# Expert layers that gather x in place with a step of eight values, x summed in PSUM, and five smaller edits

## Chip, cores and metric

One Trainium2 chip, one core. The metric is the device time of one launch in microseconds (us); lower is better. All arithmetic is float32. The program holds two layers with a mixture of experts (the first behind a convolution, the second behind an attention) and a third block with a state-space mixer, stick-breaking attention and a feed-forward network.

## The reference

The input has 256 tokens of 1024 values. The parts that the change touches, cut:

```python
ALPHA = (2.0 * DEPTH) ** 0.25            # DEPTH = 2
...
def grouped_moe(x, router_w, router_bias, w_gate, w_up, w_down):
    ...
    w = w / jnp.sum(w, -1, keepdims=True)
    gates = jnp.sum(jax.nn.one_hot(e_idx, N_EXPERTS, dtype=jnp.float32) * w[..., None], axis=1)
    def step(acc, ew):
        g_e, wg_e, wu_e, wd_e = ew
        h = jax.nn.silu(x2 @ wg_e) * (x2 @ wu_e)
        return acc + (h @ wd_e) * g_e[:, None].astype(x2.dtype), None
...
        x = layer_norm(ALPHA * x + mix, ln_mix_g[l], ln_mix_b[l])
        ffn = grouped_moe(x, router_w, router_bias, moe_w_gate[l], moe_w_up[l], moe_w_down[l])
        x = layer_norm(ALPHA * x + ffn, ln_ffn_g[l], ln_ffn_b[l])
```

There are 16 experts of width 512, and each token goes to two. The third block works on 272 positions, 16 learned ones ahead of the 256 tokens; only the tokens are put out, and its feed-forward convolution has three taps.

## The kernel before

A matmul keeps a stationary operand of up to 128x128 in TensorE (loaded by a weight load, PEld) and moves up to 512 columns past it. A float32 matmul shows in the trace as two records, each with its own weight load. `ring` is a ring of weight buffers in SBUF that the SP queue fills, `arena` is scratch, `x_nat` holds x with tokens in the partitions, `xT` the same turned. Banks 0 to 3 of PSUM go round by job (`take_bank`, `bank_free`, `job_ready`); banks 4 to 7 hold the sum over the experts. Each engine runs its own list in program order; semaphores tie them together. `normed`, `seats_ready`, `scattered` and the like are such semaphores.

**Convolution** (`conformer`). TensorE makes eight blocks of the gated product (`glu_products`, helper line 243); ScalarE writes each to DRAM (`send`, L928) and fetches it back in shifted form (`fetch_shifted`, L937, four DMAs); TensorE applies the taps (`taps`, L859) to it. Behind the last fetch, ScalarE's queue issues 17 small DMAs: the rows of the bias of the next product, router weights, and others that later stages need (L974 to L991, then `load_norm`, L496 and L498). Behind those stands `squares_of` (L951), on which TensorE's `square_part` (L876) waits. The normalization that follows works on 256 columns at a time: DVE takes a reciprocal (L522), subtracts and multiplies, ScalarE applies SiLU (L1000), and `project_and_turn` (L561) starts with the first of eight blocks.

**Routing** (`route`). TensorE makes the router's logits (L1167, L1173), DVE ranks them (L1123 to L1158) and TensorE counts places (L243 with `upto` and `ones`). Beside that ScalarE copies x twice: L1113 writes `by_row`, x with its 1024 values in another order (value 8f+k goes to place f of row k), and L1116 multiplies `x_nat` by ALPHA for the sum at the layer's end. The order is needed because the expert weights are loaded with eight rows of the matrix in each partition.

**Experts** (`experts`). The experts go in eight pairs. For a pair, `fetch` gathers its tokens: two jobs of four 128-column blocks, each block two matmuls with `by_row` as stationary operand and the seats (a 0/1 matrix of 128 tokens by 128 seats) as moving operand. So a pair's gather has 16 matmuls, 32 records and 32 weight loads. The list of one pair on TensorE is gate and up of side 0 (L1460), turning the seats (L1469), gate and up of side 1, `scatter` of the pair before (L1505, four matmuls of 512 columns), `turn` of the hidden values (L1479), gather of the next pair (L243), down (L1493). DVE's `hidden` (L1365) and ScalarE's copy of the turned values (L1428) stand between.

```python
    def gather(dst_at, tokens_dst, sources=seats):
        for c in range(4):
            k = dst_at * 4 + c
            last = products(tokens_dst[:, c * P:c * P + P],
                            [(by_row[:, t, k, :], sources[:, t, :]) for t in range(2)])
```

**Layer's end** (`ffn_norm`). DVE adds each of four 128x512 pieces of the sum to ALPHA x (`experts_sum`, L1096), takes its statistics (L1098), then centres and scales the two token tiles (L540 in layer 0, L613 and L615 in layer 1) for the transposes (L462).

**Third block.** `project_turned` (L681) multiplies 272-column operands in the z and output projections; `qk_products` (L243) makes q and k, also with 272 columns. The feed-forward stage already leaves out the first 14 positions (258 columns).

Of the kernel before, what the change touches and what calls it, by code (L numbers as in the profile page):

```python
# [24 lines left out]
F32 = mybir.dt.float32  # L25
# [23 lines left out]

IN_LAST = {x: n for n, x in enumerate(("GU0", "S", "GU1", "T", "Y0", "Y1"))}  # L50
# [13 lines left out]
FFN_TAPS = 3  # L64
OFF_XBC = D
# [81 lines left out]
def program(nc, a, out):  # L147
# [26 lines left out]
    eps_cols = sb("eps_cols", P, 2)  # L174
# [91 lines left out]
    def pair_job(layer, p, kind):  # L266
        return FJ[f"moe{layer}"] + 2 + PAIR_JOBS * p + (IN_LAST if p == PAIRS_E - 1 else IN_PAIR)[kind]

# [84 lines left out]

    block = ctx.enter_context(nc.Block())
# [5 lines left out]
    def _(sp):  # L360
# [41 lines left out]
        while u < len(units):  # L402
            src = units[u][0]
            if u == 1:

                sp.wait_ge(rows_cleared, 1)
                for q in range(QUADS):
# [4 lines left out]
                                     consts_loaded, 16)  # L412
            slot_freed(u)
# [16 lines left out]
    norm_count = [0, 0]  # L430
# [61 lines left out]
    def load_norm(k, gain, bias=None):  # L492

        act = nc.scalar
        norm_count[k % 2] += 32
        act.dma_start(norm_rows[:, k % 2, 0, :], gain.partition_broadcast(P)).then_inc(norm_loaded[k % 2], 16)  # L496
        b = gain if bias is None else bias
        act.dma_start(norm_rows[:, k % 2, 1, :], b.partition_broadcast(P)).then_inc(norm_loaded[k % 2], 16)  # L498

# [9 lines left out]
    def sqrt_of(act, values, scale, eps, table=True):  # L509
# [6 lines left out]
        bias = eps_cols[0:p, 0:1] if eps == LN_EPS else eps_cols[0:p, 1:2]  # L516
# [14 lines left out]
    def variance_of(k, t):  # L531

        nc.vector.wait_ge(stats_ready, 4 * k + 2 * t)
        nc.vector.bn_aggr(small[:, 2 * t:2 * t + 2], stats[:, t, :, :]).then_inc(var_ready, 1)

    def centred_scaled(t, root, normed, xhat=xhat):

        mean, var = mean_var(t)
        reciprocal_of(nc.vector, var, root)
        nc.vector.tensor_scalar(xhat[t - 1], x_nat[:, t, :], mean, var, ALU.subtract, ALU.mult).then_inc(normed, 1)  # L540
# [10 lines left out]
    def project_and_turn(first, u0, lhs, normed, ready=None):  # L551
# [3 lines left out]
        def part(j, half, t):  # L555
            unit_ready(u0 + half)
            take_bank(j)
            for k in range(KC):
                if ready is not None and j == first:
                    ready(k)  # L560
# [13 lines left out]
    def mix_norm(layer, normed, scaled):  # L574
# [7 lines left out]
        def _(dve):  # L582
            residual(first, 1, 0, scaled)
            residual(first + 1, 1, 1, scaled)
            variance_of(k, 1)
            centred_scaled(1, roots[0], normed)
# [3 lines left out]
            variance_of(k, 2)  # L590
            centred_scaled(2, roots[1], normed)
# [11 lines left out]
    def ffn_norm(layer, normed):  # L603
# [6 lines left out]
        def rows_out(t, root):  # L610
            dve, (mean, var) = nc.vector, mean_var(t)
            reciprocal_of(dve, var, root)
            dve_step(dve.scalar_tensor_tensor(x_nat[:, t, :], x_nat[:, t, :], mean, norm_rows[:, k % 2, 0, :],  # L613
# [5 lines left out]
        def _(dve):  # L619
            experts_sum(layer, 1, 0)  # L620
            experts_sum(layer, 1, 1)
            variance_of(k, 1)
            experts_sum(layer, 2, 0)
# [2150 lines left out]
```

## Time and profile before

| | |
|---|---|
| median of 3 runs | 1486.72 us (1485.76 to 1489.68) |
| profiled execution, its own time | 1485.41 us |
| its span, first to last instruction | 1483.7 us |
| granted TensorE clock over the span | 0.946 |
| TensorE busy / weight loads busy | 1357.4 us (91%) / 852.5 us (57%) |
| VectorE (DVE), ScalarE (ACT), GpSimd (POOL) busy | 384.4, 263.2, 24.6 us |
| share of TensorE in the chain that ended last | 88% |
| moved by DMA | 314.36 MB, mean 212 GB/s |

The profile is one execution. "Idle before" is how long an engine waited, and the arrow names what released it; "issue" is a wait for nothing that the profile shows, which can be a DMA. A matmul's busy time overlaps its neighbour's, so rates are read from the starts of merged pieces, not from mean durations.

### The profile page before, as it was taken

The numbers are of one execution on the slowest core, as the hardware profiler recorded it, in microseconds if no ns is written. First come the engines' busy times: TensorE is split into PE (matmuls) and PEld (weight loads), VectorE is DVE, ScalarE is ACT, GpSimd is POOL, SyncE is SP. The second block draws the span as 40 slices with busy tenths as digits, with TensorE's granted clock in tenths as the row PEclk, the third lists the DMA queues.
The fourth block names the chain that finished last, engine by engine and source line by source line (L and its number), as shares of the span: only waits on it lengthen the run. The fifth ranks groups of instructions, "written<-read, shape, count | busy, mean of one in ns | idle before, by whom it ended". The sixth has DMA issues, their size and how long they took to land.

```text
span 1483.7 us, 15495 instructions
## 1 busy us (share of the span) xinstructions
PE 1357.4 (91%) x6438; PEld 852.5 (57%) x6438; DVE 384.4 (26%) x857; ACT 263.2 (18%) x565; POOL 24.6 (2%) x49
## 2 busy tenths in 40 slices
PE   7979799999989978799999969988899996999997
PEld 6744434444347754434444358866686785888743
DVE  0013512112141332521112141465303205222201
ACT  1002311001102331311001121321325103000000
POOL 3110000000000000000000000000000000000000
PEclk9989799999999987799999979988999998999998
DMA  9960699999961050699999941311221033543420
GB/s 327 315 173 1 255 380 426 425 426 427 402 234 57 24 204 1 255 391 427 425 425 427 401 167 56 115 57 57 85 86 57 0 114 115 169 161 127 167 85 28
DMA packets 91663, 314.36 MB, mean 212 GB/s; under 512 B 9746, under 2 KB 47158, under 8 KB 77766
## 3 DMA queue, kind: packets, MB, share of 16 engines
q1 hardware_dynamic: 77344, 298.98, 52.0%
q10 hardware_dynamic: 14246, 14.33, 3.4%
q8 instruction: 55, 0.90, 0.3%
q14 instruction: 18, 0.15, 0.0%
HBM read 311.05 MB, written 2.24 MB: 211 GB/s over the span
## 4 chain that ended last, share of the span: by engine, by line
PE 88%; DVE 7%; DMA 1%; issue 1%; ACTq 1%; ACT 1%; DVEq 0%; SPq 0%; POOLq 0%
PE psum L243 37%; PE psum L1460 15%; PE psum L1493 8%; PE psum L681 6%; PE psum L2676 5%; PE psum L561 4%; PE psum L1505 4%; PE psum L462 1%; PE psum L859 1%; PE psum L1636 1%; PE psum L1634 1%; DMA ring<-in_a_w_pw 1%; PE psum L2334 1%; PE psum L2326 1%; PE psum L2321 1%
## 5 line engine op out<-in xcount | busy, mean ns | idle before, releaser
L243 PE MATMUL psum<-xT,ring 128*128 128x256 f32 (+2 forms) x1792 | 413.0, 392 | 8.8 <-POOLq L442 5.2
L243 PEld LDWEIGHTS psum<-xT,ring 128*128 128x128 f32 x1792 | 346.0, 194 | 72.4 <-issue 15.3
L1460 PE MATMUL psum<-ring,arena 128*64 128x512 f32 x768 | 169.6, 594 | 0.0
L1460 PEld LDWEIGHTS psum<-ring,arena 128*64 128x64 f32 x768 | 53.9, 137 | 103.9 <-issue 103.7
L243 PE MATMUL psum<-arena 128*128 128x128 f32 (+4 forms) x684 | 92.4, 291 | 1.2 <-issue 1.1
L243 PEld LDWEIGHTS psum<-arena 128*128 128x128 f32 (+2 forms) x684 | 84.1, 198 | 5.5 <-issue 4.8
L1493 PE MATMUL psum<-ring,arena 128*64 128x512 f32 x384 | 85.0, 595 | 0.0
L1365 DVE TENSOR_TENSOR arena<-psum,arena 64x512 f32<-64x512 f32 x32 | 34.3, 1073 | 191.5 <-ACT arena L1413 191.5
L2676 PE MATMUL psum<-ring,arena 128*128 128x512 f32 x176 | 75.7, 592 | 0.0
L1413 ACT ACTIVATE arena<-psum 64x512 f32<-64x512 f32 x32 | 18.9, 592 | 259.4 <-PE psum L1460 259.4
L561 PE MATMUL psum<-ring,arena 128*128 128x512 f32 x128 | 60.3, 632 | 4.5 <-ACT arena L1000 3.6
L1505 PE MATMUL psum<-arena 128*128 128x512 f32 x128 | 59.1, 605 | 1.8 <-DVE arena L1382 1.8
L681 PE MATMUL psum<-arena,ring 128*128 128x272 f32 x256 | 58.8, 392 | 0.0
L2676 PEld LDWEIGHTS psum<-ring,arena 128*128 128x128 f32 x176 | 33.4, 190 | 41.7 <-issue 41.6
L1460 PE MATMUL psum<-arena 128*64 128x512 f32 x192 | 56.6, 594 | 0.0
L462 PE MATMUL psum<-ident,arena 128*128 128x128 f32 (+1 forms) x136 | 23.3, 337 | 35.9 <-DVE arena L1835 22.2
L1493 PEld LDWEIGHTS psum<-ring,arena 128*64 128x64 f32 x384 | 26.5, 137 | 49.4 <-issue 48.0
L681 PEld LDWEIGHTS psum<-arena,ring 128*128 128x128 f32 x256 | 48.6, 190 | 10.0
L561 PEld LDWEIGHTS psum<-ring,arena 128*128 128x128 f32 x128 | 25.7, 204 | 37.0 <-issue 35.2
L1505 PEld LDWEIGHTS psum<-arena 128*128 128x128 f32 x128 | 23.0, 189 | 37.8 <-issue 34.3
L462 PEld LDWEIGHTS psum<-ident,arena 128*128 128x128 f32 (+1 forms) x136 | 20.5, 188 | 41.6 <-DVE arena L1835 23.3
L1382 DVE COPY arena<-psum 128x512 f32<-128x512 f32 x16 | 11.1, 692 | 109.4 <-PE psum L1493 109.4
(319 smaller groups left out, 1184.4 us busy)
## 6 DMA issues: line engine op xcount, KB each, us to landing
ring<-in_moe_w_gate SPq DMA_DIRECT2D x24, 2048.0 KB, 11.8
ring<-in_moe_w_up SPq DMA_DIRECT2D x24, 2048.0 KB, 15.9
ring<-in_moe_w_down SPq DMA_DIRECT2D x24, 2048.0 KB, 16.1
ring<-in_w_in SPq DMA_DIRECT2D x11, 2048.0 KB, 13.6
ring<-in_w_up SPq DMA_DIRECT2D x22, 1024.0 KB, 7.7
arena<-in_moe_w_gate SPq DMA_DIRECT2D x8, 2048.0 KB, 12.2
ring<-in_w_down SPq DMA_DIRECT2D x5, 2048.0 KB, 7.7
ring<-in_a_w_pw SPq DMA_DIRECT2D x8, 1024.0 KB, 10.9
```

The source lines that it names most:

```text
L243: last = nc.tensor.matmul(dst, lhsT, rhs, start=(n == 0), stop=(n == len(pairs) - 1))
L462: last = nc.tensor.transpose(bank(j)[:, c * P:c * P + n], src(t)[0:n, at:at + P], ident[0:n, 0:n])
L561: last = pe.matmul(bank(j), lhs(k, t), slot_k(u0 + half)[:, k, :], start=(k == 0), stop=(k == KC - 1))
L681: last = nc.tensor.matmul(bank(first + c)[:, 0:L], slot_k(part_units[half])[:, k, (c % 4) * P:(c % 4) * P + P], src[:, k, :], start=(i == ...
L859: last = pe.matmul(bank(j)[32 * g:32 * g + 32, 0:SEQ], blocks[:, c % BLOCK_BUFS, q, g, :], shifted[:, c % REP_BUFS, g, 4 * q:4 * q + SEQ], ...
L1365: dve.tensor_tensor(hid_both[part, :].rearrange("s (k f) -> s k f", f=P), by_row(bank(j)[part, :]), by_row(silu_g[part, 0, :]), ALU.mult). ...
L1413: act.activation(silu_g[UP_IN[side], 0, :], bank(j)[GATE_IN[side], :], ACT.Silu).then_inc(silu_ready, 1)
L1460: last = pe.matmul(bank(j)[part, :], tokens[:, k, side * SEATS:side * SEATS + SEATS], weights(u + n, k), start=(k == 0), stop=(k == KC - 1))
L1493: last = pe.matmul(bank(j)[part, :], hidT_both[:, k, side * SEATS:side * SEATS + SEATS], weights(u + side, k, D)[:, half * 512:half * 512 ...
L1505: last = pe.matmul(psum[:, BANKS + 2 * t + half, :], gatedT[:, p % 2, t * P:t * P + P], y_pair[:, half * 512:half * 512 + 512], start=Fals ...
L1634: pe.matmul(bank(j)[:, comp * SEQ:comp * SEQ + keys], flip, bias[:, h, SEQ - keys:SEQ], start=True, stop=False)
L2676: last = pe.matmul(psum[:, BANKS + 2 * t + half, :], fT[:, c, t * P:t * P + P], slot_k(u, D)[:, c % 4, half * 512:half * 512 + 512], start ...
```

## The change

1. **Gather in place.** `by_row` and ScalarE's copies into it are gone. The stationary operand of each gather matmul is x_nat itself with a step of eight values (32 bytes).
2. **x summed in PSUM.** In `route`, four matmuls of 512 columns with the identity put x into banks 4 to 7; the experts add to them, with gates divided by ALPHA. The copy with ALPHA and DVE's memset of the banks are gone. At the layer's end DVE reads statistics and values straight from PSUM; epsilon is divided by ALPHA squared.
3. **Order within the pairs.** In the first pair the gather of the next stands ahead of `turn`. In the last, two of the four scatter matmuls stand behind it. The last scatter takes the left halves of both tiles first, and waits for each half's copy by itself.
4. **Small DMAs.** The 17 DMAs go from ScalarE's queue to SP's, ahead of the loads of pw2, the next projection.
5. **Halves in the convolution's norm.** DVE and ScalarE work on 128 columns at a time; the second tile's columns have their own waits.
6. **Third block.** The first 14 of 272 columns are left out of z, q, the output projection and the products between.

```diff
+            if u == unit_at["pw2"]:
+                sp.dma_start(b_pw2, a["a_b_pw2"][0].partition_broadcast(P)).then_inc(bias_rows_loaded, 16)
+                sp.wait_ge(consts_made, CONSTS_MADE)
...
+                load_norm(0, a["ln_mix_g"][0], a["ln_mix_b"][0], sp)
             slot_freed(u)
...
-                                        src[:, k, :], start=(i == 0 and k == 0),
+                                        src[:, k, NEED:L], start=(i == 0 and k == 0),
...
-            for c in range(KC):
-                act.wait_ge(conv_normed, c + 1)
-                act.activation(conv[:, c, :], conv[:, c, :], ACT.Silu, bias=column("a_ln_b", c),
-                               scale=column("a_ln_g", c)).then_inc(act_ready, 1)
+            for t in range(2):
+                for c in range(KC):
+                    act.wait_ge(conv_normed, KC * t + c + 1)
+                    part = conv[:, c, t * P:t * P + P]
...
-        dve_step(dve.tensor_tensor(x_nat[:, t, cols], x_nat[:, t, cols], psum[:, BANKS + 2 * (t - 1) + half, :],
-                                   ALU.add))
-        dve.bn_stats(stats[:, t, half, :], x_nat[:, t, cols]).then_inc(stats_ready, 1)
+        dve.wait_ge(scattered, 4 * layer + 2 * half + t)
+        dve.bn_stats(stats[:, t, half, :], psum[:, BANKS + 2 * (t - 1) + half, :]).then_inc(stats_ready, 1)
...
-            for t in range(2):
-                act.wait_ge(normed[2 * layer], 3 + t)
-                act_step(act.activation(by_row[:, t, :, :], x_nat[:, t + 1, :].rearrange("p (f k) -> p k f", k=KC),
-                                        ACT.Copy))
-            act.nop().then_inc(rows_ready, 1)
-            act.activation(x_nat[:, 1:3, :], x_nat[:, 1:3, :], ACT.Copy, scale=ALPHA).then_inc(rows_ready, 1)
...
+            for t in (1, 2):
+                pe.wait_ge(normed[2 * layer], 2 + t)
+                for half in range(2):
+                    pe.matmul(psum[:, BANKS + 2 * t - 2 + half, :], ident[:, :], x_nat[:, t, half * 512:half * 512 + 512],
+                              start=True, stop=False, skip_group_check=True)
             take_bank(J + 2)
...
+            by_dim = x_nat[:, 1:3, :].rearrange("p t (f k) -> p t k f", k=KC)
             last = products(tokens_dst[:, c * P:c * P + P],
-                            [(by_row[:, t, k, :], sources[:, t, :]) for t in range(2)])
+                            [(by_dim[:, t, k, :], sources[:, t, :]) for t in range(2)])
...
-            dve.memset(psum[:, BANKS:2 * BANKS, :], 0.0).then_inc(cleared, 1)
...
-                if p == 1:
-                    pe.wait_ge(cleared, layer + 1)
-                if p > 0:
-                    scatter(p - 1)
-                turn(p)
-                if p < LAST:
-                    fetch(0, p + 1)
-                    fetch(1, p + 1)
+                if p == 0:
+                    fetch_next(p)
+                    turn(p)
+                elif p < LAST:
+                    scatter(p - 1, TOP + LOWER)
+                    turn(p)
+                    fetch_next(p)
+                else:
+                    scatter(p - 1, TOP)
+                    turn(p)
+                    scatter(p - 1, LOWER)
                 down(p)
-            scatter(LAST)
+            scatter(LAST, ((0, 0), (1, 0), (0, 1), (1, 1)))
```

How the lists move, at two places. TensorE from the router to the first pair's hidden values of layer 0 (chosen rows, in order), before (L243 is the shared helper; `arena` holds `by_row`, the seats and the tokens):

```order
L1173 MATMUL psum<-quad_diag,arena 128x16 [waits bank_free3,bank_free0]
L243 MATMUL psum<-arena,upto 128x16 [waits won_ready,bank_free2,bank_free1]
L243 MATMUL psum<-arena 128x128 [waits bank_free3,seats_ready,rows_ready]
L1460 MATMUL psum<-ring,arena 64x512 x15
L1479 MATMUL psum<-ident,arena 128x128 [waits bank_free3,bank_free1,bank_free0]
L243 MATMUL psum<-arena 128x128 [waits bank_free1,seats_ready]
```

and now:

```order
L1181 MATMUL psum<-quad_diag,arena 128x16 [waits bank_free3,bank_free0]
L1188 MATMUL psum<-x_nat,ident 128x512 [waits normed0]
L1188 MATMUL psum<-x_nat,ident 128x512
L245 MATMUL psum<-arena,upto 128x16 [waits won_ready,bank_free2,bank_free1]
L245 MATMUL psum<-arena,x_nat 128x128 [waits bank_free3,seats_ready,normed0]
L245 MATMUL psum<-arena,x_nat 128x128 [waits bank_free0,seats_ready]
L1494 MATMUL psum<-ident,arena 128x128 [waits bank_free3,bank_free1,bank_free2]
```

The identity matmuls stand ahead of the wait for `won_ready`, and the second gather ahead of the turn. ScalarE from the last fetch on, before (L974 is the first of the 17 DMAs, L951 the squares) and now (L975 the squares, L1007 SiLU):

```order
L937 DMA arena<-glu_scratch 32x4x284 x4
L974 DMA arena<-in_a_b_pw 128x1024
L976 DMA router_w<-in_router_w 128x8x16
L978 DMA router_b<-in_router_bias 128x16
L980 DMA ffn_cols<-in_ln_ffn_g 128x8x1
```

```order
L961 DMA arena<-glu_scratch 32x4x284 x4
L975 ACTIVATE arena<-arena 128x256 x8
L547 ACT_TABLE_LOAD
L553 ACTIVATE xT<-xT,eps_cols 128x256
L1002 ACT_TABLE_LOAD
L1007 ACTIVATE arena<-arena,vec 128x128 x16
```

The squares follow the last fetch directly.

## Rows read from the trace of the kernel before

**Rows 1.** Chain in order of time, layer 0, pair 1: start us, us, what.
```profile
221.81 3.63 PE psum L1505 x8
225.88 3.57 PE psum L243 x32
...
254.80 3.57 PE psum L243 x32
```
**Rows 2.** Weight loads by line and form: xcount | busy us, mean ns | idle before.
```profile
L681 PEld LDWEIGHTS psum<-arena,ring 128*128 128x128 f32 x256 | 48.6, 190 | 10.0
L1460 PEld LDWEIGHTS psum<-ring,arena 128*64 128x64 f32 x768 | 53.9, 137 | 103.9 <-issue 103.7
```
**Rows 3.** ScalarE's instructions that read x_nat: duration ns min/median/max.
```profile
L1823 ACT ACTIVATE arena<-x_nat x6: 1040/1042/1057, 862.2 to 1239.6; 128x1024 f32<-128x1024 f32 x4, 16x1024 f32<-16x1024 f32 x2
L1113 ACT ACTIVATE arena<-x_nat x4: 2041/2050/2055, 166.6 to 612.9; 128x1024 f32<-128x1024 f32 x4
```
**Rows 4.** Windows of TensorE: length, busy (records), granted clock, DMA share, GB/s.
```profile
5.00:75.00 70.00, 64.60 (x408) 1.00 1.06 328
...
166.00:171.00 5.00, 0.47 (x3) 0.50 0.98 413
...
174.00:180.00 6.00, 6.00 (x34) 0.60 0.39 156
180.00:209.00 29.00, 27.13 (x143) 1.00 0.74 297
```
**Rows 5.** Timeline of TensorE, layer 0: counting places, first gather, first turn.
```profile
171.11 0.58 PE L243 MATMUL psum<-arena,upto 128*128 128x16 f32 x2 [4.64 <-DVE arena L1149]
...
173.93 6.12 PE L243 MATMUL psum<-arena 128*128 128x128 f32 x32 [0.54 <-issue]
...
196.32 0.63 PE L1479 MATMUL psum<-ident,arena 128*128 128x128 f32 x4 [1.87 <-DVE arena L1365]
```
**Rows 6.** Chain, convolution: squares, last taps, reciprocal.
```profile
106.45 2.93 PE psum L876 x6
...
115.89 3.59 PE psum L859 x64
...
123.01 1.76 DVE xT L522
```
**Rows 7.** Squares' matmuls as a group: xcount | busy us, mean ns | idle before.
```profile
L876 PE MATMUL psum<-arena,ones 128*128 128x256 f32 x16 | 5.8, 491 | 9.9 <-ACT arena L951 9.9
```
**Rows 8.** Chain, end of layer 0's experts: copy of the last output, transposes.
```profile
407.39 0.70 DVE arena L1382
...
417.60 1.97 PE psum L462 x8
```
**Rows 9.** Timeline of TensorE, down of layer 0's last pair.
```profile
400.27 2.33 PE L1493 MATMUL psum<-arena 128*64 128x512 f32 x9 [0.89 <-ACT arena L1428]
```
**Rows 10.** Timeline of DVE at the layers' ends: statistics, one rescaling pass.
```profile
410.16 0.69 DVE L1098 BATCH_NORM_STATS2 stats<-x_nat 128x6 f32<-128x512 f32 x1
...
857.75 1.28 DVE L613 SCALAR_TENSOR_TENSOR x_nat<-x_nat,small,norm_rows 128x1024 f32<-128x1024 f32 x1
```
**Rows 11.** Chain, layer 1: copy of the last output, last rescaling pass.
```profile
851.35 0.70 DVE arena L1382
...
863.80 1.28 DVE x_nat L615
```
**Rows 12.** Chain: output projection (272 columns), feed-forward (half 258, half 256).
```profile
1166.60 58.67 PE psum L681 x256
...
1245.43 152.77 PE psum L243 x704
```
**Rows 13.** DMAs of the second block's fetch (issued 38 to 40), us to landing.
```profile
DMA to landing us min/median/max: 6.3/10.3/22.4
```
**Rows 14.** Timeline of TensorE, the taps that wait for them.
```profile
62.52 3.66 PE L859 MATMUL psum<-arena 128*32 128x256 f32 x64 [0.88 <-issue]
```
**Rows 15.** DMA of ScalarE's queue, 92 to 108: packets, MB, share of 16 engines.
```profile
q10 hardware_dynamic: 6290, 2.30, 67.9%
```

More of the change, by code:

```diff
@@ L64 @@
 FFN_TAPS = 3
+NEED = META - (FFN_TAPS - 1)
 OFF_XBC = D
@@ L558, in part @@
             for k in range(KC):
-                if ready is not None and j == first:
-                    ready(k)
+                if ready is not None and half == 0:
+                    ready(k, t)
                 last = pe.matmul(bank(j), lhs(k, t), slot_k(u0 + half)[:, k, :], start=(k == 0), stop=(k == KC - 1))
@@ L680, in project_turned @@
                     for k in range(KC):
-                        last = nc.tensor.matmul(bank(first + c)[:, 0:L],
+                        last = nc.tensor.matmul(bank(first + c)[:, NEED:L],
                                                 slot_k(part_units[half])[:, k, (c % 4) * P:(c % 4) * P + P],
-                                                src[:, k, :], start=(i == 0 and k == 0),
+                                                src[:, k, NEED:L], start=(i == 0 and k == 0),
                                                 stop=(i == len(parts) - 1 and k == KC - 1))
@@ L783, in _ @@
             pool_step(pool.memset(eps_cols[:, 1:2], EPS))
+            pool_step(pool.memset(eps_cols[:, 2:3], LN_EPS / ALPHA ** 2))
             pool.nop().then_inc(consts_made, 1)
@@ L1496, in down, with scatter, fetch_next @@
                     last.then_inc(job_done, 1)
-            def scatter(p):
+            def scatter(p, parts):
                 read_out(pe, job("S", p))
-                read_out(pe, job("Y0", p))
-                read_out(pe, job("Y1", p))
-                for t in range(2):
-                    for half in range(2):
-                        last = pe.matmul(psum[:, BANKS + 2 * t + half, :], gatedT[:, p % 2, t * P:t * P + P],
-                                         y_pair[:, half * 512:half * 512 + 512], start=False, stop=(p == LAST),
-                                         skip_group_check=True)
-                        if p == LAST:
-                            last.then_inc(scattered, 1)
-            pe.wait_ge(rows_ready, 2 * layer + 1)
+                for t, half in parts:
+                    read_out(pe, job(f"Y{half}", p))
+                    last = pe.matmul(psum[:, BANKS + 2 * t + half, :], gatedT[:, p % 2, t * P:t * P + P],
+                                     y_pair[:, half * 512:half * 512 + 512], start=False, stop=(p == LAST),
+                                     skip_group_check=True)
+                    if p == LAST:
+                        last.then_inc(scattered, 1)
+            def fetch_next(p):
+                fetch(0, p + 1)
+                fetch(1, p + 1)
+            TOP, LOWER = ((0, 0), (0, 1)), ((1, 0), (1, 1))
+            pe.wait_ge(normed[2 * layer], 4)
             fetch(0, 0)
@@ L2367, in meta_exponents @@
                 zm = psum[:, META_BANK, :]
-                pe.matmul(zm[:, 0:L], neg_from_meta[:, :, :].rearrange("p h s -> p (h s)"), soft_meta[:, g, :], start=False, stop=True,
+                pe.matmul(zm[:, NEED:L], neg_from_meta[:, :, :].rearrange("p h s -> p (h s)"), soft_meta[:, g, NEED:L], start=False, stop=True,
                           skip_group_check=True)
@@ L2598, in _ @@
         def _(pe):
-            products(psum[:, BANKS, 0:L], [(ones[:, :], sqT[:, c, :]) for c in range(KC)]).then_inc(so_summed, 1)
+            products(psum[:, BANKS, NEED:L], [(ones[:, :], sqT[:, c, NEED:L]) for c in range(KC)]).then_inc(so_summed, 1)
             w = unit_at["w_out"]
```

211 lines of the change are left out of this document (110 added, 101 removed).

## The prediction

> **What bounds the kernel.** I read the page's engine shares first: TensorE is busy for 91% of the span and makes up 88% of the chain that ended last, so most of the time is matmuls, and a stage is judged by what stands between them. In the experts, the chain runs from TensorE to TensorE: one pair takes 254.80 - 225.88 = 28.92 us, with no wait of note in it [rows 1]. DMA moves 418 to 425 GB/s there on the page, yet no matmul waits for a weight. A gather is 3.57 us of that, 32 records at 112 ns each [rows 1]. Weight loads of 128 and of 64 columns last 190 and 137 ns [rows 2], which is 0.83 ns a column, so 128 columns occupy the load path for 107 ns of the 112. In the gather, load and matmul are thus about equally long: whatever lengthens a load shows at once. In most other stretches 512 columns pass per load and cover it.
>
> **Parts that gain.**
>
> The small DMAs. TensorE waits 9.9 us for the squares on ScalarE, whose queue first issues the 17 DMAs [rows 7]. With them gone the squares follow the last fetch, and the wait goes. The first six records then took 2.93 us [rows 6] at a reduced clock; by 217 ns for such a record (152.77/704) [rows 12] they need 1.3, so another 1.6. The DMAs don't disappear: on SP's queue they stand ahead of pw2 and of the first expert weights, which aren't needed for 100 us. What they can hurt is the convolution's own traffic (a rival below). Gain 11.5 us; ends 3 and 13.
>
> Halves in the norm. The reciprocal over 256 columns takes 1.76 us [rows 6] and stands before the first product; over half of them about 0.9, and multiply and SiLU shrink by some 0.3 together. The second halves are needed some 14 us later. Gain 1.2.
>
> First pair. The turn waited 1.87 us for the hidden values [rows 5]. The gather now fills that; what becomes exposed is ScalarE's copy of the turned values, 0.89 us as it shows in the last pair [rows 9]. Gain 1.0 a layer, 2.0.
>
> Last pair. Two scatter matmuls, half of 3.63 us [rows 1], cover that 0.89 [rows 9]; the other two still cover the hidden values. Gain 0.9 a layer, 1.8.
>
> Layers' ends. Counted from the start of the last copy, layer 0 reaches the decisive transposes after 417.60 - 407.39 = 10.2 us [rows 8]. Now the scatter starts at once with left halves and ends at 3.6; 0.3 for the semaphore, one statistics pass of 0.69 [rows 10] and 0.2 to combine give 4.8. Two centring passes from PSUM at about 1.28 [rows 10], with 0.17 for each reciprocal, end at 7.7. Gain 2.5. In layer 1 four passes follow: 4.8 + 4 x 1.28 + 0.4 = 10.3, against 863.80 + 1.28 - 851.35 = 13.7 [rows 11]. Gain 3.4. Together 5.9.
>
> Third block. A record took 58.67/256 = 229 ns with 272 columns and 217 with 257 on average [rows 12], 0.81 ns a column, so 14 columns are 11.4 ns. The trimmed records are 256 in the output projection, 128 each in z and q and some 36 others. 548 x 11.4 = 6.2; a few of q stand where TensorE waits for others, so 6.0. Ends 3 and 6.5.
>
> Sum of the gains: 11.5 + 1.2 + 2.0 + 1.8 + 5.9 + 6.0 = 28.4 us.
>
> **Parts at nothing or near it.** ScalarE's two copies of x, DVE's adds and the memset were beside the ranking and the first pair. If that cover were missing, the copies would already have delayed the first gather, which waits for the seats. New are four identity matmuls a layer: 8 records, 0.43 us each at the full clock and 0.86 at half (0.84 ns a column) [rows 12], so 3.4 to 6.9 us, in an idle time of 4.64 us [rows 5] at the half clock of 1.2 GHz (granted 0.50) [rows 4]. Behind them in TensorE's list are the counting matmuls, for which the seats wait. I take a delay of 0.5 us at the first gather; ends 0 and 2.3 a layer. TensorE is busy ahead of the gather now, so I expect the full clock of 2.4 GHz in it, where it was granted 0.60 [rows 4].
>
> **The step of eight.** No weight load in this trace reads with a step. From below its cost is nothing. The nearest rows are ScalarE's, on the same tensor with the same step: 1024 values in 2050 ns, against 1042 in order [rows 3]. That is 0.98 ns more a value, 128 x 0.98 = 126 ns a load. From above, the load might not only be longer but also stop overlapping its neighbour: 190 [rows 2] + 126 = 316 ns a record. I take the middle: the load path is occupied for 107 + 126 = 233 ns, with 2 for the handover 235 a record, since ScalarE too reads a value in 0.8 ns in order, at about the rate of the load. A gather becomes 32 x 235 = 7.5 us, 3.95 more. Of the 16, 14 stand in the full-clock chain: 55.3. The two first ones took 6.12 [rows 5] and start 0.5 later: 1.9 each, 3.8. Together 59.1 us, and nothing covers it, since the down products need the same TensorE.
>
> The Trainium skill ("SBUF — State Buffer", in the section on the DMA port swizzle) speaks against this change: SBUF is read in 16-byte lines, and an access that goes to a new line each time pays. By it, a step of 32 bytes pays on every value; it gives no price for a weight load, and ScalarE's row agrees with it.
>
> Sum against the profiled execution: 1485.4 - 28.4 + 59.1 = 1516.1. The median of the runs is 1.3 above that execution, so **1517 us**.
>
> **Rivals.**
>
> A: loads don't care about the step. What speaks for it: weight loads keep a rate of 0.83 ns a column over several shapes [rows 2], as if the array and not the memory set it, and TensorE may fetch ahead. Against: ScalarE's ratio of two. Then gathers stay at 3.57, and the two first ones gain the clock, 6.12 to 3.57 less 0.5, 2.0 each: 1485.4 - 28.4 - 4.1 + 1.3 = 1454 us. This is the other side; the point is a gather of 3.57 + 28.4/14 = 5.6 us, or 175 ns a record. Below it the kernel is faster. The Trainium skill ("TensorE: Matmul & The Clock Gate", section "LDWEIGHTS (loading the stationary operand)") gives a load as columns / 1.2 in ns, with nothing for the step; the slope in order agrees, and by it the time would be this rival's.
>
> B: the moved DMAs come back as waits. From 5 to 75 us the DMA engines are full (share 1.06) [rows 4]; the fetches of the second block land after up to 22.4 us [rows 13], and the taps behind them already wait 0.88 [rows 14]. In their old place ScalarE's DMAs took 67.9% of 16 us [rows 15], 10.9, about 8 of it the small ones. If those 8 land on the second block's taps, the convolution keeps only 5 of its 12.7: with the step's cost 1525 us. Against: most fetches have room, and the large loads move behind them.
>
> C: the loads no longer overlap, 316 ns a record: 10.1 us a gather, 92 for 14 and 9 for the first two, 42 more than forecast: 1559 us. A clock that falls during a sparse gather, so that the down products behind start at 1.2 GHz, would end in the same region. Against both: the loads of the present gather overlap, and no wait stands in it.
>
> D: the step costs a part, below 175 ns a record: 1460 to 1500.
>
> **Chances and range.** A measurement of this kernel can tell about 0.3% from no change, 4.5 us. Forecast 0.57 (its own range, from gains of 20 to 32 and a step's cost of 50 to 64: 1504 to 1530), A 0.22, B 0.09, C 0.06, D 0.06. Faster: A and half of D, 0.25. Same: 0.02, of D. Slower: 0.73. To leave out no more than 2 in 10 the range must reach to A and to B: 1448 to 1532.
>
> **What would show it.** Right: the gather's pieces of 32 records at 7.5 us in both layers; weight loads there at about 316 ns where others stay at 190; a pair of 32.9 us. The squares' wait of 9.9 gone, the squares at 96 to 97 us; layer 0's experts end 2.5 us sooner after the last copy; output projection at 218 ns a record, 55.8 us in all. Wrong: gathers at 3.6 us (A), a wait before the second block's taps of several us (B), gathers of 10 us or a granted clock below 1.00 between 180 and 400 us (C).

## The result and the profile after

| | before | changed |
|---|---|---|
| median | 1486.84 us (4 runs, 1485.76 to 1489.68) | 1514.52 us (4 runs, 1510.30 to 1517.53) |
| profiled execution, its own time | 1485.41 us | 1517.28 us |
| its span | 1483.7 us | 1515.6 us |
| granted TensorE clock | 0.946 | 0.959 |
| TensorE / weight loads busy | 1357.4 / 852.5 us | 1412.9 / 912.6 us |

The changed kernel takes 1.0181 of the time before (95% interval 1.0147 to 1.0215), so it is slower by 1.5 to 2.2%. The medians are 27.7 us apart. The changed kernel's profiled execution is 2.8 us above its median and the other 1.4 below, so the two spans, which what follows compares, are 31.9 us apart.

Weight loads as a group: xcount | busy us, mean ns | idle before. Loads of the same size in the third block's projections (L715) still take 190 ns, as in [rows 2].

```profile
L245 PEld LDWEIGHTS psum<-arena,x_nat 128*128 128x128 f32 x512 | 123.0, 335 | 3.6 <-issue 3.6
```

The chain that ended last, layer 0, pairs 1 and 2 (start us, us, what). It answers to [rows 1].

```profile
219.39 3.63 PE psum L1518 x8
223.46 7.61 PE psum L245 x32
...
256.41 7.61 PE psum L245 x32
```

A gather is 7.61 us, 238 ns a record, instead of 3.57 and 112. A pair is 256.41 - 223.46 = 32.95 us. The scatter keeps its 3.63. So the whole of the pair's growth of 4.03 us is the gather.

TensorE's timeline in the convolution (in brackets: idle before, and what released it). L883 is the taps, L900 the squares' matmuls, L597 the product that follows. It answers to [rows 6], [rows 7] and [rows 14].

```profile
82.16 3.66 PE L883 MATMUL psum<-arena 128*32 128x256 f32 x64
87.18 3.66 PE L883 MATMUL psum<-arena 128*32 128x256 f32 x64 [1.36 <-issue]
...
96.05 6.50 PE L883 MATMUL psum<-arena 128*32 128x256 f32 x64 [3.29 <-issue]
102.48 1.56 PE L900 MATMUL psum<-arena,ones 128*128 128x256 f32 x6
...
119.06 6.16 PE L597 MATMUL psum<-ring,arena 128*128 128x512 f32 x10 [2.59 <-ACT arena L1007]
```

The squares' wait of 9.9 us is gone, and so is the second block's 0.88. But the fifth and sixth taps now wait 1.36 and 3.29 us, and the sixth runs 6.50 instead of 3.66. The window of TensorE around it (length, busy, granted clock, DMA share, GB/s) shows half the clock, 1.2 GHz, after that wait:

```profile
95.00:100.00 5.00, 3.95 (x40) 2.21 (x44) 0.17 (x1) 0.71 (x3) 0.00 (x0) 0.50 0.54 140
```

The view of DMAs shows what the taps wait for. For the fetches issued between 62 and 82 us it has (xcount, KB each, median us to landing), and for the queue of SP's loads in the same stretch (packets, MB, share of 16 engines), first changed:

```profile
arena<-glu_scratch ACTq DMA_DIRECT2D x8, 142.0 KB, 18.3
q1 hardware_dynamic: 810, 6.99, 92.0%
```

and before:

```profile
arena<-glu_scratch ACTq DMA_DIRECT2D x12, 142.0 KB, 7.8
q1 hardware_dynamic: 145, 2.10, 30.0%
```

The fetches take more than twice as long, in a stretch in which SP's queue now moves 6.99 MB instead of 2.10.

TensorE's timeline in layer 0's routing: the identity matmuls, the first counting matmuls, the first two gathers [rows 5].

```profile
158.80 5.91 PE L1188 MATMUL psum<-x_nat,ident 128*128 128x512 f32 x8
164.54 0.29 PE L245 MATMUL psum<-arena,upto 128*128 128x16 f32 x2
...
166.66 7.84 PE L245 MATMUL psum<-arena,x_nat 128*128 128x128 f32 x32 [0.94 <-issue]
...
188.84 7.87 PE L245 MATMUL psum<-arena,x_nat 128*128 128x128 f32 x32
```

The chain at the layers' ends and in the third block. It answers to [rows 8], [rows 11] and [rows 12].

```profile
428.34 2.79 PE psum L1518 x6
433.01 1.34 DVE arena L576
434.46 1.35 DVE arena L576
436.28 3.59 PE psum L505 x16
439.88 41.51 PE psum L245 x128
...
902.31 2.79 PE psum L1518 x6
...
911.02 1.28 DVE x_nat L651
913.20 4.62 PE psum L505 x24
919.08 28.08 PE psum L715 x128
...
1201.37 55.68 PE psum L715 x256
...
1277.32 152.77 PE psum L245 x704
```

With the same events of before, the span divides like this. The forecast column is the prediction's terms put where they belong.

| stretch | before | changed | difference | forecast |
|---|---|---|---|---|
| to the first product after the convolution | 126.00 | 119.06 | -6.9 | -12.7 |
| from there to the first gather | 47.93 | 47.60 | -0.3 | +0.5 |
| first gather to v (layer 0's experts) | 245.64 | 273.22 | +27.6 | +24.7 |
| attention | 151.06 | 152.26 | +1.2 | 0 |
| layer 1's routing | 47.49 | 48.49 | +1.0 | +0.5 |
| first gather to z (layer 1's experts) | 253.77 | 278.45 | +24.7 | +23.8 |
| z to the feed-forward | 373.54 | 358.24 | -15.3 | -6.0 |
| the rest | 238.3 | 238.3 | 0 | 0 |

The parts sum to 32.0 against a forecast of 30.7 (59.1 - 28.4), but three rows are off by 3 to 9 us and largely cancel. The experiments are about these three and about the gather; attention's 1.2 us stay unexplained.

### The profile page after: what moved, and what is told of

It is laid out like the page before. It is cut to its first block, busy times and chain, and to the rows that moved or that the text cites. A ratio compares the mean times of both kernels' runs of the same rounds, so it can differ in the third digit from the quotient of the medians.

```text
span 1515.6 us, 15533 instructions
## 1 busy us (share of the span) xinstructions
PE 1412.9 (93%) x6454; PEld 912.6 (60%) x6454; DVE 378.5 (25%) x864; ACT 254.1 (17%) x569; POOL 25.1 (2%) x50
## 4 chain that ended last, share of the span: by engine, by line
PE 91%; DVE 5%; issue 1%; ACT 1%; DMA 1%; DVEq 0%; ACTq 0%; SPq 0%; POOLq 0%
PE psum L245 39%; PE psum L1475 15%; PE psum L1508 7%; PE psum L715 6%; PE psum L2700 5%; PE psum L597 4%; PE psum L1518 4%; PE psum L883 2%; PE psum L505 1%; PE psum L1658 1%; PE psum L1656 1%; PE psum L1188 1%; DMA ring<-in_a_w_pw 1%; PE psum L2358 1%; PE psum L2350 1%
## 5 line engine op out<-in xcount | busy, mean ns | idle before, releaser
L245 PE MATMUL psum<-xT,ring 128*128 128x256 f32 (+2 forms) x1792 | 405.5, 388 | 8.8 <-POOLq L485 5.2
L245 PEld LDWEIGHTS psum<-xT,ring 128*128 128x128 f32 x1792 | 342.5, 192 | 68.0 <-issue 15.0
L245 PE MATMUL psum<-arena,x_nat 128*128 128x128 f32 x512 | 124.7, 404 | 1.9 <-issue 1.9
L245 PEld LDWEIGHTS psum<-arena,x_nat 128*128 128x128 f32 x512 | 123.0, 335 | 3.6 <-issue 3.6
L597 PE MATMUL psum<-ring,arena 128*128 128x512 f32 x128 | 59.7, 627 | 3.4 <-ACT arena L1007 2.6
L715 PE MATMUL psum<-arena,ring 128*128 128x258 f32 x256 | 55.8, 382 | 0.0
L505 PE MATMUL psum<-ident,arena 128*128 128x128 f32 (+1 forms) x136 | 23.6, 343 | 33.3 <-DVE arena L1857 19.1
L715 PEld LDWEIGHTS psum<-arena,ring 128*128 128x128 f32 x256 | 48.7, 190 | 6.9
L597 PEld LDWEIGHTS psum<-ring,arena 128*128 128x128 f32 x128 | 25.6, 203 | 35.5 <-issue 34.0
L505 PEld LDWEIGHTS psum<-ident,arena 128*128 128x128 f32 (+1 forms) x136 | 20.9, 190 | 38.7 <-DVE arena L1857 20.2
```

The costliest lines, as they stand in the source:

```text
L245: last = nc.tensor.matmul(dst, lhsT, rhs, start=(n == 0), stop=(n == len(pairs) - 1))
L505: last = nc.tensor.transpose(bank(j)[:, c * P:c * P + n], src(t)[0:n, at:at + P], ident[0:n, 0:n])
L597: last = pe.matmul(bank(j), lhs(k, t), slot_k(u0 + half)[:, k, :], start=(k == 0), stop=(k == KC - 1))
L715: last = nc.tensor.matmul(bank(first + c)[:, NEED:L], slot_k(part_units[half])[:, k, (c % 4) * P:(c % 4) * P + P], src[:, k, NEED:L], star ...
```

## Experiments

### The step, alone and in three sizes

The kernel before, with `by_row` laid out so that the gather's stationary operand has a step of STEP values; x stays in `by_row`, and ScalarE still copies, in STEP passes a tile instead of one. Nothing else changes.

```diff
-                            [(by_row[:, t, k, :], sources[:, t, :]) for t in range(2)])
+                            [(by_row[:, t, :].rearrange("p (ks f kk) -> p ks f kk", f=P, kk=STEP)[
+                                :, k // STEP, :, k % STEP], sources[:, t, :]) for t in range(2)])
```

> The kernel before with one edit: by_row keeps x in natural order (value 8f+k stays at place 8f+k), and the gather reads its stationary operand there with a step of eight values. ScalarE's copies stay. Theory (the step itself makes the load path longer): weight loads of the gather at about 335 ns, gathers of 7.6 us, first ones 7.9, pair of 32.9 us, 14 x 4.04 + 2 x 1.8 = 60 us above the kernel before, 1547 us. Rival 1 (what the changed kernel shows comes from another of its edits, such as x standing in x_nat or the new order in the pairs): gathers below 5 us here and less than 25 us above the kernel before. Rival 2 (the step costs, but part of it was hidden in the changed kernel by its new order): more than 65 us above.

> The kernel before with by_row laid out in groups of four, so that the gather reads with a step of four values (16 bytes). By lines of 16 bytes, every value is on a line of its own, as at eight: gathers 7.6 us, 238 ns a record, about 1547 us. If the price grows with the distance, it is half of it: about 175 ns a record, 5.6 us, about 1516 us. If it is a price on each pass over 32 bytes alone: 3.6 us and about 1487 us.

> The same with a step of two values (8 bytes), so that two values stand on each line of 16 bytes. By the rule that an access is slow when less than two values of a line are used: gathers at 3.6 us, no change, about 1487 us. If every non-unit step pays in full: 7.6 us, 1547 us. If the price is per line touched (64 lines for 128 values, against 32 in order and 128 at a step of four): a third of the whole, about 154 ns a record, 4.9 us, about 1507 us.

The chain's row of pair 1's gather (start us, us), with a step of two:

```profile
226.35 3.77 PE psum L243 x32
```

the same row with a step of four:

```profile
229.46 7.46 PE psum L243 x32
```

and with a step of eight:

```profile
231.70 7.61 PE psum L243 x32
```

| step | bytes | ns a record | time |
|---|---|---|---|
| 1 (before) | 4 | 112 | 1486.04 us (7 runs beside these) |
| 2 | 8 | 118 | 1489.11 us (1 run) |
| 4 | 16 | 233 | 1541.25 us (1 run) |
| 8 | 32 | 238 | 1549.15 us, ratio 1.0426 (1.0407 to 1.0445) |

The price is a stair, not a slope: almost nothing at 8 bytes, nearly all of it at 16, and 5 ns more at 32. The rivals "grows with the distance" (175 ns expected at 16 bytes), "over 32 bytes alone" (112 at 16) and "each non-unit step" (238 ns at 8) fall, and the price per line touched (154 ns at 8) falls as well. No step of 12 bytes was run, so the riser lies somewhere between 8 and 16. The single runs of four and two values tell little by their times, but their gathers are plain in the traces. The Trainium skill ("SBUF — State Buffer", in the section on the DMA port swizzle) asks for at least two hits on each 16-byte line. The four sizes agree with it, now for a weight load: two values on a line cost 118 ns a record, one value 233. The same place says that a float32 access can stride four values for free; here the measurement differs, since four values cost 233 ns, and it decides. The step alone costs 63 us, which the interval (60.5 to 66.1) can't tell from the 60 expected. ScalarE's eight passes a tile took 7.0 us a layer instead of 4.1 and delayed the first gather by a quarter of a microsecond, which is a cost of this experiment and not of the step.

### The gather in order again

The changed kernel with ScalarE's copy and `by_row` back, all other edits kept.

```diff
+            for t in range(2):
+                act.wait_ge(normed[2 * layer], 3 + t)
+                act_step(act.activation(by_row[:, t, :, :], x_nat[:, t + 1, :].rearrange("p (f k) -> p k f", k=KC),
+                                        ACT.Copy))
+            act.nop().then_inc(rows_ready, 1)
...
-                            [(by_dim[:, t, k, :], sources[:, t, :]) for t in range(2)])
+                            [(by_row[:, t, k, :], sources[:, t, :]) for t in range(2)])
```

> The changed kernel with one part undone: ScalarE's copy into by_row is back and the gather reads it in order; x summed in PSUM, the order in the pairs, the moved DMAs and the third block stay. Theory: gathers back at 3.57 us, and since the copies (2 x 2.05 us a layer on ScalarE) lie beside the ranking, all of 14 x 4.04 + 2 x 1.8 = 60 us comes back: 1454 to 1456 us, 31 to 33 us faster than the kernel before. Rival (the copies, now beside four identity matmuls and the ranking, delay the first gather): as above but 2 to 4 us later in each layer, 1458 to 1463 us.

1451.88 us (1449.0 to 1455.45), ratio 0.9772 (0.9748 to 0.9796). Against the changed kernel's 1.0181 that is 4.1% of 1486, 61 us, within 6 us either way by the two intervals, for 60 expected. The gather in pair 1 (chain):

```profile
212.10 3.57 PE psum L245 x32
```

Its first gathers take 3.81 us, not the 6.12 and 5.91 of before ([rows 5] has the first): TensorE is busy with the identity matmuls ahead of them, and the clock granted in layer 0's is 1.00 instead of 0.60. ScalarE's copies delay nothing. The traces thus put the step at 14 x 4.04 + 2 x 4.03 = 64.6 us here and at 60.2 against the kernel before; the medians allow both. The 4.4 us between them are a gain of the identity matmuls that the step hides. With it, the first gather takes 7.84 us at a clock of 1.00 in the changed kernel and 7.91 at 0.69 in step8_alone: while the loads set the pace, the clock is worth nothing there. So the step costs what the prediction said, or a little more, and everything else in the change gains about 34 us (30 to 37).

### Where the small DMAs go

Two variants of this kernel, unit_gather. In one the DMAs stand on ScalarE's queue again, in the other on SP's queue, but behind pw2 and the first four expert loads, from 83 us on instead of 24. (Kernel and trace have 16 of them; the 17 of the earlier sections is one too many.)

```diff
-            if u == unit_at["pw2"]:
+            if u == unit_at["moe0"] + 4:
                 sp.dma_start(b_pw2, a["a_b_pw2"][0].partition_broadcast(P)).then_inc(bias_rows_loaded, 16)
```

> unit_gather with one more part undone: the 17 small DMAs stand on ScalarE's queue again, behind the last fetch and ahead of the squares. Theory (the move gains what the traces show, the squares' wait less what comes back at the taps): TensorE waits about 9 to 10 us for the squares again, no wait of over 1 us ahead of the taps, the first product at about 125 us against 119.1 in the changed kernel and 116.0 in unit_gather; 6 to 9 us slower than unit_gather, 1458 to 1461 us. Rival (the full 11.5 us of the prediction were gained, and something else in the convolution lost them): the same waits as in the kernel before, but 11 to 12 us slower, 1463 us, with the first product at 127 us or later.

> unit_gather with the 17 small DMAs on SP's queue two loads of matrices later: behind the four expert loads that the ring takes, from 82 us on, instead of ahead of pw2 at 24 us. Theory (8 us of small DMAs in the stretch where the DMA engines are full push the fetches of the convolution back, and this is the wait ahead of the taps): the waits of 1.4 to 3.3 us ahead of the fifth and sixth taps shrink below 1 us, the squares start by 97 us, the first product at 112 to 114 us, 2 to 4 us faster than unit_gather, 1448 to 1450 us. Rival 1 (the fetches wait for the expert loads, not for the small DMAs): waits ahead of the taps stay, no change. Rival 2: the small ones land after 112 us and TensorE waits for them ahead of the first product: slower by some us.

TensorE's timeline in unit_gather, the sixth taps:

```profile
94.11 5.35 PE L883 MATMUL psum<-arena 128*32 128x256 f32 x64 [2.61 <-issue]
```

with the DMAs back on ScalarE (L880 is the squares, L577 the first product):

```profile
104.49 2.93 PE L880 MATMUL psum<-arena,ones 128*128 128x256 f32 x6 [9.52 <-ACT arena L955]
...
123.40 12.04 PE L577 MATMUL psum<-ring,arena 128*128 128x512 f32 x24 [2.59 <-ACT arena L1006]
```

and with them late on SP:

```profile
91.95 3.66 PE L883 MATMUL psum<-arena 128*32 128x256 f32 x64
97.29 1.56 PE L900 MATMUL psum<-arena,ones 128*128 128x256 f32 x6 [1.68 <-ACT arena L975]
...
113.86 21.68 PE L597 MATMUL psum<-ring,arena 128*128 128x512 f32 x46 [2.59 <-ACT arena L1007]
```

| | first product | wait ahead of taps | median, ratio |
|---|---|---|---|
| changed kernel | 119.06 | 1.36, 3.29 | |
| unit_gather | 115.96 | 0.31, 2.61 | 1451.88, 0.9772 |
| back on ScalarE | 123.40 | none | 1457.41, 0.9812 (0.9786 to 0.9838) |
| late on SP | 113.86 | none | 1450.43, 0.9747 (0.9723 to 0.9772) |

Back: the squares' wait returns with 9.52 us and the taps' waits go. The kernel is 5.5 us slower by the medians (5.9 by the ratios), at the low edge of the 6 to 9 expected; the intervals of the two ratios overlap, so the traces carry this reading: the first product comes 7.4 us later. Late: no wait ahead of the taps, squares at 97.29, and the fetches of the same stretch land after 7.8 us again. That shows that the place of the small DMAs is the cause. How they push the fetches back is read from the traces and not tested by itself: in the changed kernel pw2's loads start 19 us later than before, the first two expert loads 13 and 9, and they run beside the fetches that land late. The 2.1 us that it gains over unit_gather in the trace can't be told from nothing in the medians. The length of the taps' wait moves between runs of the same list (3.1 us at the first product between the changed kernel and unit_gather, which have the same list up to there).

### The end of layer 0

First the order of DVE's passes, and of the last scatter with it, since the prediction had them decide:

```diff
+            if layer == 0:
+                for t in (1, 2):
+                    experts_stats(layer, t, 0)
+                    experts_stats(layer, t, 1)
+                    variance_of(k, t, 2 * t)
+                    centred_scaled(t, roots[t - 1], normed, layer_sum(t), xhat_ffn[t - 1])
```

> unit_gather with the end of layer 0 alone in the old order: the last scatter goes tile by tile, and DVE takes statistics and centres the first tile before it takes the second. Layer 1 keeps the halves. Theory (in layer 0 the new order puts both centring passes, 2 x 1.35 us, and all 16 transposes, 3.6 us, behind the last scatter; by tiles, half of each lies beside it): from the end of the last down product to the first product of v, 11.7 us in unit_gather, about 9 us here; 2 to 3 us faster, 1449 us. Rival (the prediction's step holds, the order by halves is worth 2.5 us and the transposes lose it by their clock alone): 2 to 3 us slower, 1454 us.

DVE's timeline, the first centring (L576):

```profile
393.54 1.34 DVE L576 TENSOR_SCALAR arena<-psum,small 128x1024 f32<-128x1024 f32 x1
```

and the chain from there (L505 is the transposes):

```profile
394.90 3.17 issue
398.07 3.65 PE psum L505 x16
```

No change: 1450.17 us, ratio 0.9758 (0.9732 to 0.9783). DVE is done with the first tile at 394.88, and TensorE starts its transposes at 398.07. Both theories fell here. Counted from the first matmul of the last scatter, the transposes start after 8.06 us (398.07 - 390.01), in unit_gather after 8.07, in the changed kernel after 8.01 (436.28 - 428.27), whatever DVE does. Counted from the end of the last down product it is 7.9 to 8.0 us in these, and 8.2 in the kernel before, where the scatter itself starts 0.88 us late. What stands on TensorE in between is the reading of a count of tokens beyond the seats, and a branch on it, which is not entered. In the kernel before, only the first eight transposes start at this time. DVE's timeline there, and TensorE's:

```profile
413.79 0.81 DVE L540 TENSOR_SCALAR arena<-x_nat,small 128x1024 f32<-128x1024 f32 x1
...
416.73 0.81 DVE L540 TENSOR_SCALAR arena<-x_nat,small 128x1024 f32<-128x1024 f32 x1
```

```profile
415.55 4.02 PE L462 MATMUL psum<-ident,arena 128*128 128x128 f32 x16 [3.65 <-DVE arena L540]
```

The first tile is centred at 414.60, and its transposes start 0.95 us later; the second is centred at 417.54, and its eight start at 417.60 [rows 8], released by DVE.

Three more kernels, on top of small_dmas_late, test reading and branch. One leaves both out on all engines in layer 0, one reads the count early (below), and one does that with layer 0's end by tiles:

```diff
                 down(p)
+                if p == 2:
+                    load_count(pe, layer)
...
-            load_count(pe, layer)
```

> small_dmas_late with the overflow part of layer 0 left out on all engines: the reading of the count of tokens beyond the seats, the branch on it and the loop that it guards (not entered on these inputs). Theory (at the end of layer 0 TensorE doesn't wait for DVE: in the kernel before, the changed one, unit_gather and layer0_end_by_tiles its transposes all start 8.0 to 8.2 us after the last down product ends, whatever DVE's order, since between the last scatter and them it reads the count and takes the branch): the transposes start once the first centring pass is done, about 6.3 us after the last down product's end, and v's first product 9.5 to 10 us after it instead of 11.7; about 2 us faster. Rival (DVE's centring sets the start, as the profile's arrow says): 8.0 and 11.7 us as before.

> small_dmas_late with TensorE's reading of the overflow count moved from behind the last scatter to behind the third pair's down products, in both layers; the branch stays. If the reading is what takes the time: the transposes of layer 0 start about 6.3 us after the last down product's end instead of 8.0, v's first product at 9.5 to 10, and the reading costs nothing or up to 2 us at the third pair. If the branch itself takes it: no change at the end, 8.0 and 11.7 us. 1448 to 1450 us either way, so the trace decides.

> count_read_early with layer 0's end by tiles as in layer0_end_by_tiles. If the reading was in the way: now the order of the passes shows, the first tile's transposes start about 5 us after the last down product's end and those of the second at 8.4, v's first product at about 9.5 us; with the late small DMAs 1446 to 1449 us, the fastest of the study, ratio to the kernel before about 0.973. If the branch is in the way: 8.0 and 11.7 us again, 1450 us.

TensorE's timeline, the transposes, in small_dmas_late:

```profile
399.02 3.65 PE L505 MATMUL psum<-ident,arena 128*128 128x128 f32 x16 [4.36 <-DVE arena L576]
```

without reading and branch:

```profile
397.74 3.63 PE L505 MATMUL psum<-ident,arena 128*128 128x128 f32 x16 [2.44 <-DVE arena L576]
```

with the reading early:

```profile
396.73 3.65 PE L505 MATMUL psum<-ident,arena 128*128 128x128 f32 x16 [3.49 <-issue]
```

and the same by tiles:

```profile
397.10 3.65 PE L505 MATMUL psum<-ident,arena 128*128 128x128 f32 x16 [3.47 <-issue]
```

| | scatter to transposes | idle before them | median, ratio |
|---|---|---|---|
| small_dmas_late | 8.05 | 4.36 | 1450.43, 0.9747 |
| no reading, no branch | 6.14 | 2.44 | 1448.02, one run |
| reading early | 7.19 | 3.49 | 1449.68, 0.9756 (0.9736 to 0.9776) |
| reading early, by tiles | 7.18 | 3.47 | 1450.81, 0.9759 (0.9742 to 0.9776) |

The reading at the end costs 0.87 us of idle time. The end of what is left, 3.49 us, is set by the branch, since it stays when DVE is done with the first tile 2.3 us before (by tiles) and falls to 2.44 when the branch is gone; those 2.44 are DVE's. Together reading and branch hold the transposes back by 1.9 us here (8.05 - 6.14). So each of the two explanations expected for the early reading holds a part. None of this moves the whole time by more than its measurement can tell. In small_dmas_late the arrow of the profile names DVE's centring; among the kernels with the new order it is right only in the one without the branch, where the transposes start 0.05 us after the first centring pass ends.

### The third block

The kernel before with the trimmed columns alone, for example:

```diff
-        products(psum[:, BANKS + n % 4, 0:L], [(slot_k(u)[:, k, (n % 4) * P:(n % 4) * P + P], xT[:, k, :])
-                                               for k in range(KC)]).then_inc(qk_done, 1)
+        at = NEED if n < KC else 0
+        products(psum[:, BANKS + n % 4, at:L], [(slot_k(u)[:, k, (n % 4) * P:(n % 4) * P + P], xT[:, k, at:L])
+                                                for k in range(KC)]).then_inc(qk_done, 1)
```

> The kernel before with the third block's edit alone: the first 14 of 272 columns left out of z, q, the output projection and the products between. Theory (only the 548 shorter records count, the rest of the 15 us that the changed kernel's third block gained is the clock granted in that run): 6 us below the kernel before, 1480 us, ratio 0.996. Rival (the edit itself brings 15 us, since shorter records let ScalarE and DVE catch up or move the clock): 1471 us, ratio 0.990.

1474.44 us, ratio 0.9920 (0.9898 to 0.9942): 12 us faster, 9 to 15. It is twice the 6 us of the shorter records, and closer to the rival. From z to the feed-forward it takes 363.26 us. Over all kernels of this study, that stretch is 371.95 to 373.84 us in the four with 272 columns and 358.24 to 363.26 in the nine with 258. So the gain comes with the edit and not with the run, 12.0 us on average. TensorE's timeline shows two places where the surplus over the shorter records arises. The first, before:

```profile
949.60 4.33 PE L243 MATMUL psum<-w_dt,xT 128*16 128x16 f32 x48
953.77 12.85 PE L243 MATMUL psum<-xT,ring 128*128 128x272 f32 x48
```

and trimmed:

```profile
946.90 4.24 PE L244 MATMUL psum<-w_dt,xT 128*16 128x16 f32 x48
950.99 10.69 PE L244 MATMUL psum<-xT,ring 128*128 128x258 f32 x48
```

The window behind the 16-column matmuls has the granted clock (the third number from the end), before:

```profile
953.70:959.70 6.00, 6.00 (x21) 4.78 (x21) 3.71 (x15) 5.29 (x10) 0.00 (x0) 0.72 0.53 203
```

and trimmed:

```profile
951.00:957.00 6.00, 6.00 (x30) 5.26 (x30) 3.71 (x15) 5.19 (x10) 0.00 (x0) 1.00 0.53 201
```

Fourteen columns on 48 records are 48 x 11.4 ns = 0.55 us; the piece shrinks by 2.16. The other 1.6 is the clock, granted 0.72 before and 1.00 now, behind the same 48 matmuls of 16 columns. It is 0.72 or 0.73 there in all four kernels of 272 columns and 1.00 in all nine of 258; the chain's merged piece that holds both groups is 60.97 us in the four and 58.72 in the nine. The second place is 40 us on, before:

```profile
995.75 8.61 PE L243 MATMUL psum<-xT,ring 128*128 128x272 f32 x32
```

and trimmed:

```profile
990.01 7.12 PE L244 MATMUL psum<-xT,ring 128*128 128x258 f32 x32
```

The columns are 0.37 us of these 1.49, and the granted clock in the stretch that leads into the piece (993 to 998, and 988 to 992.5) is 0.66 before and 1.00 now. The rest of the surplus isn't located. Why shorter records keep the clock up isn't shown by these runs either.

## Why the prediction was right, and where it wasn't

The forecast was 1517 us, slower; it is 1514.5. The case it called likeliest happened, and for its main reason.

- **The step.** 235 ns a record and 32.9 us a pair forecast, 238 ns and 32.95 us measured; loads at 335 ns where 316 were expected. The first gathers took 7.84 and 7.85 us, 1.7 and 1.9 more than before, for 1.4 forecast. In all 60.2 us in the trace (14 x 4.04 + 1.72 + 1.94) and about 61 between the runs, for 58.1 forecast, or 59.1 with the two later starts. Taking ScalarE's price for a step of eight over to the weight load, and adding it to the path of a load, gave the right size. It was a middle between two bounds and an analogy, though: no row of before showed a weight load with a step. Rivals A and D fell, and C too: the clock in the pairs stays at 1.00.
- **Small DMAs, 11.5 us.** Mis-sized. The prediction subtracted the squares' wait in full and gave rival B, that the moved transfers come back as waits, only 0.09. It came, as a part: 6.9 us gained in the trace of the convolution with the norm's 1.0 in it, thus 5.9 of 11.5. It came at the fifth and sixth taps, not at the second block's: that block's fetches, late before, now landed sooner, while those issued between 62 and 82 us landed after 18.3 us instead of 7.8. "The large loads move behind them" was the weak point: pushed back by the 18 us that SP took to issue the small ones (23.60 to 42.05 in the trace), they met the later fetches, with 6.99 MB on SP's queue in that stretch instead of 2.10.
- **Halves in the norm, 1.2 us.** 1.04: the wait ahead of the first product went from 3.63 to 2.59 us.
- **Identity matmuls, a delay of 0.5 us.** They took 5.91 us in layer 0, mostly at half the clock. In unit_gather, which has the same list there, the counting starts 0.9 us after DVE's last ranking step instead of 0.15, but DVE has its first result after 0.84 us instead of 1.54, at the higher clock. So layer 0 lost nothing; layer 1 lost about 1.
- **First pair 1.0 a layer, last pair 0.9.** The time from the first gather's end to the first down product grew by 3.05 us, which is the second gather's 4.04 less 1.0. In the last pair the time from the gather's start to the down product grew by 4.04 less 0.73.
- **End of layer 0, 2.5 us.** Wrong step: 0.7 gained (from the end of the last down product to v, 12.2 us became 11.5). DVE's part was right: the second centring pass ends 7.5 us after that point, for 7.7 forecast. What the prediction had wrong is that DVE alone decides and that only the second tile's eight transposes stand behind it, as in [rows 8]. TensorE's reading and branch hold it until 7.9 us, and all 16 transposes stand behind that now. Without them, v starts 9.7 us after the last down product, which is what the prediction's sum gives (7.7 and 2.0 for eight transposes).
- **End of layer 1, 3.4 us.** 3.8. Four longer passes of DVE outlast the branch there, so what the edits save on DVE shows in full. Which of them it is (the adds that are gone, the order by halves, the scatter without its wait) was not separated.
- **Third block, 6.0 us.** Mis-sized by half: 12 us by the edit alone in the runs, 15.3 in the changed kernel's profiled execution. The changed kernel's 358.24 us is the shortest of the nine trimmed ones. The width of the records was priced rightly, 55.68 us for the output projection against 55.8 forecast. What the sum lacked is that the granted clock moves with the edit; about 3 us of the surplus are traced to it, the rest is open.

Gains that fell short by 5.6 and 1.8 us and one that was larger by about 9 nearly cancel, so it is luck that the total is better than its terms. The direction didn't hang on them.

## What to carry over

Look at the step, in bytes, of every operand that an engine reads on the critical path: in this gather, where the load is as long as the matmul, a step of 16 or 32 bytes doubles the time of a record and a step of 8 bytes doesn't, and a copy on an idle engine that puts the operand in order is worth far more than it costs (here about 61 us for nothing on the path). Undo one part of a bundle before rejecting it: without the step, the rest gains some 34 us together. When a wait is taken from one queue by moving transfers to another, look at what lands in the stretch where they now run, and look for a place where the DMA engines have room.

## What was not expected of the hardware

- A gather bound by TensorE's weight loads (128x128 float32) follows a stair: 112, 118, 233 and 238 ns a record for steps of 4, 8, 16 and 32 bytes. At 32 bytes it takes the same time at a granted clock of 0.69 as at 1.00 (7.91 and 7.84 us).
- Reading a count into TensorE's register and branching on it, not entered, kept TensorE from its next matmul until 8 us after the last down product, with 4.36 us idle. Without them it was 2.44, and DVE's; with the reading earlier, 3.49. None of it carries the branch's name in the profile.
- 14 columns less in the records of a stretch kept the granted clock at 1.00 in a place where it fell to 0.72 or 0.73 in every kernel with the longer records.
